# A decoder trunk on one core: the slots of the high- and low-weight rings made 32 bytes longer

## The reference

```python
for i in range(DEPTH):                        # DEPTH = 2
    mod = c_act @ w_mod[i] + b_mod[i]
    sh1, sc1, g1, sh2, sc2, g2 = jnp.split(mod, N_MOD, axis=-1)
    h = modulate(x, norm1_w[i], sh1, sc1)
    if i % N_MIXERS == 0:
        y = hgrn2_mixer(h, ...)               # h @ w_in (1024x4096), recurrence, @ w_out
    else:
        y = fox_mixer(h, ...)                 # h @ w_in (1024x4112), attention, @ w_out
    x = x + g1[:, None, :] * y
    h = modulate(x, norm2_w[i], sh2, sc2)
    x = x + g2[:, None, :] * sqrelu_mlp(h, w1[i], w2[i])   # 1024 -> 4096 -> 1024
return rmsnorm(x, final_w)
```

## The kernel before

| tensors | address modulo 128 bytes |
|---|---|
| `x`, `raw`, `whi`, `wlo` | 0 |
| layer 0: `h0`, `y0`, `h1`, `a0` (both parts), `hq`, `hk`, `wfhi`, `wflo` | 64 |
| layer 1: `h2`, `y1`, `h3`, `a1` (both parts), `qt`, `kt` | 0 |
| `ident` | 96 |

## Time and profile before

### The profile page before, as it was taken

One profiled execution on the slowest core, in us unless ns is written; L12 is line 12 of the kernel. 1 busy time (PEld: TensorE's weight loads), 2 busy tenths in 40 slices (PEclk: granted clock), 3 DMA queues, 4 the chain that ended last, 5 costly groups with the idle time before them and its releaser, 6 DMA issues.

```text
span 1490.3 us, 20799 instructions
## 1 busy us (share of the span) xinstructions
PE 1416.5 (95%) x7488; PEld 1186.5 (80%) x7488; DVE 753.5 (51%) x1087; ACT 506.8 (34%) x750; POOL 687.3 (46%) x399
## 2 busy tenths in 40 slices
PE   2789999999899999999998999999989999999997
PEld 2678988988788888888787888888778888888885
DVE  7764656464698457871253333333356541255312
ACT  3513232313343223332245353534234332233220
POOL 8456758474355455554434333333053444444440
PEclk9889999999899999999999999999999999999998
DMA  9233433322265456542323121211032223222221
GB/s 380 101 141 114 141 114 118 137 72 70 87 225 197 169 181 214 197 165 89 99 68 103 57 86 57 86 58 57 15 104 80 89 95 99 85 99 99 85 70 57
DMA packets 46192, 169.83 MB, mean 114 GB/s; under 512 B 5024, under 2 KB 5152, under 8 KB 45360
## 3 DMA queue, kind: packets, MB, share of 16 engines
q1 hardware_dynamic: 45520, 164.73, 32.0%
q10 hardware_dynamic: 608, 4.23, 0.8%
HBM read 166.81 MB, written 2.13 MB: 113 GB/s over the span
## 4 chain that ended last, share of the span: by engine, by line
PE 66%; issue 19%; POOL 8%; DVE 5%; ACT 1%; DMA 1%; POOLq 0%; DVEq 0%; ACTq 0%; SPq 0%
PE bank L624 13%; PE bank L625 13%; PE bank L626 13%; POOL wlo L547 8%; PE bank L679 4%; PE bank L681 4%; PE bank L680 4%; PE bank L752 3%; PE bank L894 3%; PE bank L918 2%; PE bank L771 1%; PE bank L905 1%; DVE modf L1073 1%; PE bank L896 1%; DVE mring L1033 1%
## 5 line engine op out<-in xcount | busy, mean ns | idle before, releaser
L547 POOL TENSOR_TENSOR wlo<-raw,whi 128x1024 fp32r<-128x1024 f32 x208 | 539.2, 2596 | 661.5 <-ACT whi L287 661.5
L287 ACT ACTIVATE whi<-raw 128x1024 fp32r<-128x1024 f32 x204 | 215.1, 1055 | 211.3 <-PE bank L626 187.5
L1178 DVE SCALAR_TENSOR_TENSOR x<-bank,mod,x 128x512 f32<-128x512 f32 (+1 forms) x48 | 35.9, 749 | 234.6 <-PE bank L626 234.6
L1033 DVE CUSTOM_DVE_ANT_0 mring<-mring,cb 128x1024 f32<-128x1024 f32 x80 | 124.9, 1570 | 4.0 <-DMA mring<-mod_rows 4.0
L679 PE MATMUL bank<-whi,h2hi 128*128 128x256 f32 x384 | 111.3, 290 | 0.0
L1266 DVE CUSTOM_DVE_ANT_0 scr<-bank,fb 128x128 f32<-128x128 f32 (+1 forms) x64 | 31.1, 486 | 153.7 <-issue 153.7
L681 PE MATMUL bank<-wlo,h2hi 128*128 128x256 f32 x384 | 108.5, 283 | 0.0
L680 PE MATMUL bank<-whi,h2lo 128*128 128x256 f32 x384 | 108.4, 282 | 0.0
L398 ACT ACTIVATE scr<-bank 128x512 f32<-128x512 f32 x64 | 38.2, 597 | 196.4 <-PE bank L626 196.4
L624 PE MATMUL bank<-h3hi,whi 128*128 128x512 f32 x256 | 102.1, 399 | 2.4 <-issue 2.4
L624 PE MATMUL bank<-h1hi,whi 128*128 128x512 f32 x256 | 100.9, 394 | 2.4 <-DVE h1lo L1013 2.4
(11 more groups left out here) (231 smaller groups left out, 3158.3 us busy)
## 6 DMA issues: line engine op xcount, KB each, us to landing
raw<-stream SPq DMA_DIRECT2D x208, 512.0 KB, 3.5
mring<-mod_rows SPq DMA_DIRECT2D x80, 512.0 KB, 3.5
modf<-mod_rows SPq DMA_DIRECT2D x8, 1024.0 KB, 18.1
fb<-negf ACTq DMA_DIRECT2D x4, 1024.0 KB, 5.5
x<-x_t SPq DMA_DIRECT2D x2, 1024.0 KB, 7.0
out_t<-x SPq DMA_DIRECT2D x8, 256.0 KB, 2.1
cb<-c_row SPq DMA_DIRECT2D x1, 512.0 KB, 4.1
wf<-w_forget SPq DMA_DIRECT2D x1, 512.0 KB, 4.3
```

What stands on the lines that cost most here:

```text
L287: S.activation(whi[:, j, :], raw[:, j, :], ACT.Copy).then_inc(w_hi, 1)
L547: G.tensor_tensor(wlo[:, j, :], raw[:, j, :], whi[:, j, :].bitcast(F32), ALU.subtract).then_inc(w_lo, 1)
L1033: V.tensor_tensor_reduce(out=mring[:, s, :], in0=mring[:, s, :], in1=cb[:, :], scale=1.0, scalar=0.0, op0=ALU.mult, op1=ALU.add, accum_out ...
```

## The change

Each slot of `whi` and `wlo` gets eight floats more at its end, and the copies that fill the slots name the first 1024 floats. The matmuls take their columns as before.

```diff
+SKEW = 8
...
-        whi = sb("whi", [P, 4, D], F32R)
-        wlo = sb("wlo", [P, 4, D], F32R)
+        whi = sb("whi", [P, 4, D + SKEW], F32R)
+        wlo = sb("wlo", [P, 4, D + SKEW], F32R)
...
-                S.activation(whi[:, j, :], raw[:, j, :], ACT.Copy).then_inc(w_hi, 1)
+                S.activation(whi[:, j, 0:D], raw[:, j, :], ACT.Copy).then_inc(w_hi, 1)
...
-                G.tensor_tensor(wlo[:, j, :], raw[:, j, :], whi[:, j, :].bitcast(F32), ALU.subtract).then_inc(w_lo, 1)
+                G.tensor_tensor(wlo[:, j, 0:D], raw[:, j, :], whi[:, j, 0:D].bitcast(F32), ALU.subtract).then_inc(w_lo, 1)
```

## The result

The changed kernel takes 1502.64 us (median of 11 runs, 1501.67 to 1505.74) against 1496.47 us for the kernel before on the same chip (11 runs, 1492.48 to 1501.50). The ratio is 1.0039, with a 95% interval of 1.0028 to 1.0051: slower by 0.39%, or about 6 us. The forecast was 1491.8 us, with 1486.5 to 1501.5 as range.

What follows compares the result with a forecast made beforehand. TensorE's matmul pace was taken to bound the kernel; +2.2 - 1.8 - 3.3 - 1.7 = -4.6 us took the span from 1490.3 to 1485.7, and the median, 6.1 higher, to 1491.8 us, range 1486.5 to 1501.5.

Steps and rivals of the forecast that it cites:

- What bounds the kernel: TensorE in the MLPs: busy 100.00 of 100 us, never fed too late, so only the pace of matmuls counts.
- Two paces come from the operands' places: MLP matmuls: 228.9 ns in layer 0 with operands 64 apart, 232.3 ns in layer 1 with equal places modulo 128.
- the four distances of the forget gate: Layer 1, weights at 64 and activations at 0: 0.91 us for four matmuls, 228 ns each, layer 0's pace.
- modulo 128: Moving and stationary operands beginning at the same place modulo 128 hinder each other: 5.576 us a block against 5.493, 0.083 more.
- slot 0 stays as it is in both layers: Feature blocks in slot 0 keep distance 64 in layer 0 and 0 in layer 1, so no cost or gain.
- The rival that names a larger multiple of 128: Layers differ for another reason, or wlo and whi lie a multiple of more than 128 bytes away: zero, 1496.4 us; chance 0.12.
- The price of 32 and 96: Feature blocks at these distances, 48 in layer 0 and 40 in layer 1, take 228.9 ns a matmul; layer 1 gains 3.3 us.
- The rows on `ident`: Transposes at distance 96 take 273 ns against 275 for matmuls with equal places, taken as support for a good price there.
- The sum: Feature and token blocks on TensorE's path: +2.2 - 1.8 - 3.3 - 1.7 = -4.6 us.
- -3.0 for the two: Feature blocks of both layers: +2.2 us in layer 0's slot 2, -1.8 and -3.3 us in layer 1.
- Token blocks: In layer 1, 16 of 24 leave distance 0 at 0.106 us each, -1.7 us; in layer 0 none comes to 0.
- The slower rival: Only 64 is good, 32 and 96 hinder as much as 0: layer 0 +6.2, layer 1 -1.8, 1500.7 us; chance 0.20.

Runs made afterwards that it cites:

- ring_at_64: Kernel before with whi and wlo 64 bytes further and everything after them 256 bytes further; 1481.37 us, ratio 0.9908.
- wlo_128: Kernel before, slots not lengthened, with wlo 128 bytes further and everything after it 256 bytes further; 1501.48 us against 1495.45, ratio 1.0038.
- skew_wlo_256: The changed kernel with wlo a further 128 bytes on, 256 against before, and everything after it moved by 512; ratio 1.0011.
- rest_256: Kernel before with only what is declared after wlo moved, by 256 bytes; 1495.51 us in one execution, beside a median of 1496.0 for before.
- hi_lo_apart_64: Kernel before with whi starting 64 bytes further and wlo 256 bytes further; 1500.41 us in one execution.
- wlo_128_not_read: As wlo_128, but the third product of feature blocks reads whi where it read wlo; 1497.96 us in one execution (before 1496.2).
- best_with_h0: Kernel before with whi and wlo 64 bytes further, layer 1's MLP tensors a further 192, h0 and y0 of layer 0 a further 64; 1478.07 us, ratio 0.9884.

## Why the prediction was wrong, point by point

- **What bounds the kernel** was right. TensorE is busy for all of the MLPs before and after, the filling of the slots kept its duration to 0.3%, and all of the effect is in the pace of matmuls.
- **Two paces come from the operands' places**: right. ring_at_64 gave layer 1 the pace of layer 0 by moving the weights. The rule that the prediction weighed against this and read as "no effect", the Trainium skill's page "SBUF — State Buffer", section "A bandwidth-pool intuition that's wrong (but worth ruling out)", which gives the weight load a read port of its own, would by that reading have had one pace in all of these runs. The measured 226.7 to 233.3 ns decide against reading it as "places do not matter". One of the prediction's supports was weaker than it says: the four distances of the forget gate that it reads as 228 ns are 229.5 ns in the unrounded trace, and all 18 back-to-back ones of that stretch average 230.7 ns, midway between the paces of the two layers.
- **The step that failed** is the reading of those paces "modulo 128", as a nuisance at equal places. The trace of before held two distances, 64 and 128 modulo 256, and I called the second one 0. The runs have 256 as the turn, and real equality of places is the best case, not the worst (5.440 us). With that, "slot 0 stays as it is in both layers" was wrong: `wlo` had moved by 128 bytes, which the layout shows (the diff makes `whi` 128 bytes longer) and the prediction passed over. The rival that names a larger multiple of 128 priced it at zero, taking it for a reason why nothing would happen. In its place wlo_128 shows 6.0 us for that move alone, and skew_wlo_256, where it is undone modulo 256, a ratio of 1.0011.
- **The price of 32 and 96**: taken as 228.9 ns, measured as 233.3. This term alone would have been wrong by 88 blocks x 0.107 = 9.4 us. The rows on `ident`, another kind of matmul, were no guide, and nothing else on record stood behind the choice.
- **The sum.** By the measured blocks: layer 0 22 x 0.098 + 22 x 0.089 + 26 x 0.058 + 26 x 0.096 = +8.1 us, layer 1 18 x 0.032 + 18 x 0.025 + 22 x 0.017 + 22 x 0.011 = +1.6, where the prediction had -3.0 for the two. Token blocks moved by -0.7 us (117.5 for 116.8 ns with `h0`, 118.1 for 119.0 with `h2`, 384 and 1152 matmuls), predicted -1.7 (from 117.8 ns for a run that by its rows took 2.83 us / 24 = 117.9). That makes +9.0 us against 6.2 measured (4.2 to 7.6 by the interval). The two MLPs by themselves, first matmul to last, grew by 5.9 us against rest_256 (354.3 to 358.8 and 359.1 to 360.7), so about the whole measured loss lies there. Most of the difference between the sum and the measurement is in the mixer of layer 0: from the first matmul with `h0` to the last with `y0` it took 350.3 us, in rest_256 349.2, so 1.1 us more, where 32 blocks at their new prices would bring 2.7. There TensorE also waits for others. That the rest lies in waits too was not tested.
- **The slower rival** had the right size for 32 and 96 (it took 232.3 ns; its 74 x 0.083 is 6.1, not 6.2, and its total stands) and came to 1500.7, near the 1502.64 measured, but by a mechanism that does not exist: it still kept slot 0 for free and 64 as good. In the changed kernel no block keeps the price of one distance, as its two parts lie 128 bytes apart.

## What to carry to other kernels

Where TensorE is busy without a gap, the distance between the start of matmuls is worth reading to the nanosecond: two layers with the same code and different paces are a layout to be mended, here worth 1.2% by a few unused floats. Before spreading operands over places, move a whole buffer by 32, 64 and 128 bytes and read the pace of each, since the good distance was a single one of those tried and a spread pays for the bad ones. And when a buffer is made longer, count what it does to the place of everything declared behind it.

## What the runs showed of the hardware

- Two paces hold from matmul to matmul, at granted clock 1.00: 226.67 ns at distance 0 and 233.33 ns at distance 192, which is 544 and 560 clocks of 2.4 GHz for 512 columns. Those of the token blocks, 113.3 and 120.0 ns, are 272 and 288 clocks for 256 columns: 16 clocks apart each time. The others are means over short patterns of unequal distances: 228.9 ns over 226, 229 and 232, and the 233.3 ns of distances 32 and 96 over such as 231, 232 and 237. 233.3 ns is not the upper end: hi_lo_apart_64 has 234.1 ns in layer 1.
- At distance 64 the pace is not one number. In wlo_128_not_read three quarters of layer 0's MLP had 228.9 ns and the first 233.3 ns. The forget gate, at distance 64 in every kernel here, averaged 229.0 ns in best_with_h0 and 230.7 in the kernel before. And with `wlo` 128 bytes off the two executions of one program differ by quarter. A quarter is 16 blocks, so one quarter at the other pace is worth 16 x 0.107 = 1.7 us. Distance 0 had 226.7 ns in every block of the MLPs, once past the start of a quarter, in all four runs that have it in all slots.
- Why the turn is 256 bytes, and whether it is the load of the next stationary operand or that of the one in use that meets the stream, no run here tells. wlo_128_not_read shows only that the loads from `wlo` are part of it.
